# Evacuating L, T and Q of the RWKV chunk inverse with one VectorE operation over two PSUM banks

## What is computed

```python
def wkv7(r, decay, k, v, kk, a):          # per head: state is 64 x 64
    def step(state, inp):
        r_t, w_t, k_t, v_t, kk_t, a_t = inp
        sa = jnp.einsum('bhvk,bhk->bhv', state, kk_t)
        state = (state * w_t[:, :, None, :]
                 - sa[..., None] * (kk_t * a_t)[:, :, None, :]
                 + v_t[..., None] * k_t[:, :, None, :])
        y = jnp.einsum('bhvk,bhk->bhv', state, r_t)
        return state, y
```

## Time and profile before

| what | us |
|---|---|
| median of 3 runs | 4954.84 |
| lowest and highest | 4953.95, 4960.62 |
| the profiled execution | 4947.15 |
| its span, first to last instruction | 4945.4 |
| PE busy in it | 4560.1 |
| DVE busy in it | 1713.5 |
| ACT busy in it | 1292.5 |
| POOL busy in it | 339.9 |

### The profile page before, as it was taken

One profiled execution on the slowest core, in us unless ns is written; L12 is line 12 of the kernel. 1 busy time (PEld: TensorE's weight loads), 2 busy tenths in 40 slices (PEclk: granted clock), 3 DMA queues, 4 the chain that ended last, 5 costly groups with the idle time before them and its releaser, 6 DMA issues.

```text
span 4945.4 us, 91370 instructions
## 1 busy us (share of the span) xinstructions
PE 4560.1 (92%) x36311; PEld 2445.3 (49%) x36311; DVE 1713.5 (35%) x3522; ACT 1292.5 (26%) x2794; POOL 339.9 (7%) x466
## 2 busy tenths in 40 slices
PE   6999999999999999999999998994999999999992
PEld 4455555555555555555555555453444444444440
DVE  3334444444444344344344344224111111111115
ACT  4222332332232333323323332431111111111115
POOL 0000000000000000000000000000000000000004
PEclk8999999999999999999999999996999999999996
DMA  8101001001001001001001002333788888888887
GB/s 295 50 5 47 10 8 47 10 8 47 10 10 45 10 12 43 10 12 45 8 12 45 8 12 69 107 123 132 281 330 335 339 330 340 333 330 343 330 322 296
DMA packets 252843, 637.03 MB, mean 129 GB/s; under 512 B 11026, under 2 KB 96244, under 8 KB 252532
## 3 DMA queue, kind: packets, MB, share of 16 engines
q1 hardware_dynamic: 238852, 582.26, 32.3%
q0 software_dynamic: 13680, 49.81, 2.6%
HBM read 563.32 MB, written 68.71 MB: 128 GB/s over the span
## 4 chain that ended last, share of the span: by engine, by line
PE 88%; issue 4%; DVE 3%; DMA 2%; SPq 1%; POOL 1%; ACT 1%; DVEq 0%; POOLq 0%; ACTq 0%
PE bank L892 36%; PE bank L1216 18%; PE bank L1235 9%; PE bank L1104 5%; PE duo L1015 4%; PE duo L1002 2%; PE duo L1004 2%; PE bank L933 1%; PE duo L1205 1%; PE duo L984 1%; PE bank L947 1%; PE duo L829 1%; DMA yb<-y_s,dix 1%; DVE LTb L1847 1%; PE duo L1156 1%
## 5 line engine op out<-in xcount | busy, mean ns | idle before, releaser
L892 PE MATMUL bank<-hT,w 128*128 (+1 forms) x4096 | 1790.5, 594 | 0.0
L892 PEld LDWEIGHTS bank<-hT,w 128*128 128x128 f32 x4096 | 777.9, 191 | 994.0 <-issue 994.0
L1216 PE MATMUL bank<-WI,xT 128*128 128x512 f32 x2016 | 877.8, 594 | 2.4 <-DVE xT L2068 2.4
L1216 PEld LDWEIGHTS bank<-WI,xT 128*128 128x128 f32 x2016 | 379.2, 191 | 455.9 <-issue 455.9
L1235 PE MATMUL bank<-WO,aT 128*128 128x512 f32 x1008 | 443.1, 593 | 1.0 <-DVE ysb L2085 1.0
L1262 ACT ACT_TABLE_LOAD x268 | 343.8, 1283 | 20.9 <-DVE ub L1812 14.3
L2074 DVE TENSOR_TENSOR gsig<-bank,gsig 128x512 f32<-128x512 f32 x63 | 43.6, 692 | 847.6 <-ACT gsig L1262 847.6
L1235 PEld LDWEIGHTS bank<-WO,aT 128*128 128x128 f32 x1008 | 186.8, 190 | 212.5 <-issue 211.2
L1262 ACT ACTIVATE gsig<-bank 128x512 f32<-128x512 f32 x63 | 37.6, 598 | 827.8 <-PE bank L1216 827.8
L1015 PE MATMUL duo<-Qm,Zm 64*64 64x64 f32 x5120 | 203.6, 227 | 36.4 <-issue 29.6
L659 POOL TENSOR_TENSOR Tm<-Tm,idents 128x512 f32<-128x512 f32 x32 | 40.6, 1268 | 2842.9 <-DVE Tm L1845 2842.9
(11 more groups left out here) (338 smaller groups left out, 5313.2 us busy)
## 6 DMA issues: line engine op xcount, KB each, us to landing
WI<-in_w_expert_in_dram SPq DMA_DIRECT2D x63, 4096.0 KB, 17.0
WO<-in_w_expert_out_dram SPq DMA_DIRECT2D x63, 2048.0 KB, 7.9
w<-in_w_in_dram SPq DMA_DIRECT2D x64, 512.0 KB, 3.9
y_s<-ysb SPq DMA_DIRECT2D x63, 512.0 KB, 17.7
adaw<-in_w_ada_dram SPq DMA_DIRECT2D x12, 2048.0 KB, 13.0
xt<-in_x_dram SPq DMA_DIRECT2D x16, 512.0 KB, 9.2
WAc<-rank_s SPq DMA_DIRECT2D x32, 256.0 KB, 3.2
GDc<-rank_s SPq DMA_DIRECT2D x32, 256.0 KB, 3.2
```

Of the source, the lines that this page charges most:

```text
L892: ins = mm(PJ[j % 2][:, :], w[:, j, k, :], hT[:, k, ds(group(i) * G, G)], start=k == 0, stop=k == KT - 1)
L1216: ins = mm(GU[j][:, :], xT[:, s, k, :], WI[:, s, k, j * DE:j * DE + DE], start=k == 0, stop=k == KT - 1)
```

## The change

`evacuate` keeps only LT and GK. L, Z, T and Q go through a new `evacuate_both`, one operation of 128x512 over both banks, which signals by adding 2. A hop behind the product is then made by the general clause, that is behind the whole evacuation.

```diff
                 def evacuate(kind, lv, b):
                     u = (kind, lv, b, 0)
                     wait_gram(dve, i, u)
...
-                    if kind == "L":
-                        ins = V.tensor_tensor(Tm[:, cs, :], bk, over(m0s[:, :], 4), ALU.mult)
...
-                    elif kind == "T":
-                        ins = V.tensor_tensor(Tm[:, cs, :], Tm[:, cs, :], bk, ALU.subtract)
                     else:
-                        ins = V.tensor_tensor(Qm[p][:, cs, :], Qm[p][:, cs, :], bk, ALU.subtract)
-                    ins.then_inc(S["gram_evac"], 1)
...
+                def evacuate_both(kind, lv):
+                    u = (kind, lv, 1, 0)
+                    wait_gram(dve, i, u)
+                    bk = DUO[pair_of(u)][:, :, 0:4 * HD].rearrange("p b (c t) -> p b c t", t=HD)
+                    to = {"L": Tm, "Z": Zm, "T": Tm, "Q": Qm[p]}[kind][:, :, :].rearrange("p (b c) t -> p b c t", b=2)
+                    if kind in ("L", "Z"):
...
+                        ins = V.tensor_tensor(to, to, bk, ALU.subtract)
+                    ins.then_inc(S["gram_evac"], 2)
...
-                        if name == "Z":
-                            evacuate_Z(more[0])
+                        if name not in ("LT", "GK"):
+                            evacuate_both(name, more[0])
                         else:
                             evacuate(name, more[0], 0)
                             if SCHED[n + 1][0] == "hop":
```

More of the change, by code:

```diff
@@ L1841, in evacuate @@
                     wait_gram(dve, i, u)
-                    bk = bank(u)[:, 0:4 * HD].rearrange("p (c t) -> p c t", t=HD)
-                    cs = slice(4 * b, 4 * b + 4)
-                    if kind == "L":
-                        ins = V.tensor_tensor(Tm[:, cs, :], bk, over(m0s[:, :], 4), ALU.mult)
[L1846 to L1849, removed]
-                    elif kind == "T":
-                        ins = V.tensor_tensor(Tm[:, cs, :], Tm[:, cs, :], bk, ALU.subtract)
-                    else:
-                        ins = V.tensor_tensor(Qm[p][:, cs, :], Qm[p][:, cs, :], bk, ALU.subtract)
@@ L1854, in evacuate @@
-                    ins.then_inc(S["gram_evac"], 1)
[L1856 to L1862, removed]
+                    V.tensor_tensor((LTb if kind == "LT" else GKb)[p][:, 4 * b:4 * b + 4, :],
+                                    bank(u)[:, :].rearrange("p (c t) -> p c t", t=P),
+                                    over(mN[:, :], 4), ALU.mult).then_inc(S["gram_evac"], 1)
@@ new lines, in evacuate_both @@
+                def evacuate_both(kind, lv):
[4 more added lines that the diff above has]
+                    if kind in ("L", "Z"):
+                        mask = m0s[:, :] if kind == "L" else mlevs[:, lv - 1, :]
+                        ins = V.tensor_tensor(to, bk, mask.unsqueeze(1).unsqueeze(1).to_broadcast([P, 2, 4, HD]),
+                                              ALU.mult)
+                    else:
+                        ins = V.tensor_tensor(to, to, bk, ALU.subtract)
+                    ins.then_inc(S["gram_evac"], 2)
```

## The result

| what | before | after |
|---|---|---|
| median, us | 4956.56 (18 runs) | 4968.77 (18 runs) |
| lowest to highest, us | 4948.46 to 4960.62 | 4960.64 to 4978.54 |
| the profiled execution, us | 4947.15 | 4966.49 |
| DVE busy, us | 1713.5 | 1680.4 |
| PE busy, us | 4560.1 | 4558.5 |

The ratio is 1.0027, with a 95% interval of 1.0021 to 1.0034: 12 us slower, where 15 were forecast. On another chip the same kernel came out at 1.0041 [1.0028, 1.0054]. VectorE has 33 us less to do, and the kernel is slower by a quarter of a per cent or more.

A forecast was written before the change was run, and what follows sets the result against it. PE was taken to bound the kernel, waiting for hops' `xs` rather than evacuations. Terms 0.26 + 0.23 + 0 - 0.01 = 0.48 us a step, over 31 steps 14.9 us, put the median at 4970 (+0.3%), range 4957 to 4981.

The forecast's parts named there:

- Place 1, L/x0: Hop x0 behind L's evacuation: u0 waits for `xs`, so it starts 0.26 us later; term 0.26 us a step.
- That the delay stays: From u0 through LT to u1: DVE has no pause up to `xs` of x1, so the whole chain moves by 0.26.
- Place 5, Q3/x5: Hop x5 behind Q3's evacuation: u5 bound, +0.27, partly refunded by a gap; term 0.23 between 0.04 and 0.27.
- T4's gap: "Issue" gap of 0.23 us in product T4; if it ends at a fixed time, T4 and x6 move less.
- Places 2, 3, 4, 6, 7: Hops at T1/x2, Q2/sy3, T3/sy4, T4/x6 and Q5/sy7: slack or cover, term 0 each; T4/x6 bounded by 0 and 0.26.
- the pairs without a hop: Three merged pairs with no hop between: each saves 0.06 us on DVE, given 0.01 together.
- place 6: Hop x6 behind T4's evacuation: u6 held by Q4 if place 5 made that late; term 0, bounds 0 and 0.26.
- The gaps take it back: Rival: PE's "issue" gaps shorten and refund half of the delay, no measurable change, 4962.5 us; chance 0.22.
- More places are bound: Rival: places 2, 3 and 6 join where gaps fall otherwise, 25 us slower, 4980 us; chance 0.16.
- The saved cost counts: Rival: PE waits for DVE's evacuations, so 320 pairs by 0.06 give 19 us less, 4936 us; chance 0.05.
- Step 0: The step without hops: gains at most ten times 0.06 us, left out of the sum.

The follow-up runs named there:

- hop_first: The changed kernel, but with the hop put ahead of the merged evacuation at L/x0, Q3/x5 and T4/x6; ratio to the kernel before 0.9987 [0.9978, 0.9996].
- merge_others: The changed kernel, but with halves and the hop between them at L/x0 and Q3/x5 only; ratio to the kernel before 0.9998 [0.9989, 1.0007].
- merge_nohop: The changed kernel, but merged at T2, Q1 and Q4 alone, with halves and the hop between at the seven places; ratio to the kernel before 0.9991 [0.9982, 1.0].
- before_add_one: The kernel before the change, with Z's evacuation adding 1 to its semaphore in place of 2; 4933.29 against 4940.14 us, ratio 0.9983 [0.9974, 0.9992].

## Why the prediction was right, and where its sizes were off

- **What bounds.** Right. `xs` is what PE waits for, and the saving on DVE was no time: its busy time fell and the kernel became slower.
- **Place 1, L/x0.** Right place, mis-sized term: 0.37 for 0.26. The part that was worked out from rows holds: u0 came 1.06 us behind the start of L's evacuation (1.05 forecast), `xs` of x1 4.71 behind it (4.74 forecast). What failed is the silent assumption that the merged operation starts when the half did. It waits for the second signal (0.03 to 0.04) and for the separate wait instruction that comes with adding 2 (0.07).
- **That the delay stays.** Right result, by a chain that was not complete. "From there DVE has no pause" is true in the rows, but the length of DVE's seeds is set by GpSimd's. For a delay it made little difference (0.37 at `xs` of x0, 0.33 at that of x1): L's evacuation is also complete sooner, 1.55 in place of 1.90, and GpSimd's work on T with it. GpSimd's first seed then starts 0.24 us later and DVE's 0.37, so that DVE's is hardly held and takes 0.42 us in place of 0.45, which is the 0.03. For a gain it would have been wrong: hop_first lost all of it there.
- **Place 5, Q3/x5.** Right, mis-sized: from x5 to u5 it is 1.25 us in place of 0.87, so +0.38 where the sum had 0.23 between 0.04 and 0.27. The refund that I expected from T4's gap isn't there (u5 +0.79, Q4 +0.78), and the upper bound of 0.27 was too low for the same reason as at place 1.
- **Places 2, 3, 4, 6, 7 and the pairs without a hop.** Right, by merge_others and merge_nohop. `xs` of x4 still stood 0.73 us behind Z3's evacuation, and x4 alone was late. u6 starts 0.86 us behind the start of Q4 before and after, so it is Q4 that holds it. The condition that I gave, that place 5 has already made Q4 late, is needed: in merge_others, where it hasn't, place 6 costs 0.09.
- **The sum.** 0.48 a step was forecast, 0.78 measured in the profiled execution and 0.65 in its repetition (31.37 less 30.72), which by 31 steps is 24 and 20 us. That the forecast time fits the first median so closely (4970 for 4968.77) is partly luck: the sum was too small, and something outside the steps' table made up for it. In the profiled execution this is the start, faster by 4.4 us, and the dense parts, by 2.0 (1893.1 in place of 1895.1); for the medians it isn't shown. The second comparison, 18.4 us, is the one that comes near the table. Why the two medians' differences, 12.2 and 18.4, are apart isn't settled.
- **DVE's busy time** fell by 33 us and not by 46. I took 320 times 0.14 from durations alone. But three pairs of ten stand back to back and save 0.06 each, as my own part on the edit's cost says: 96 by 0.06 and 224 by 0.14 are 37 us. The two numbers of the prediction contradicted each other.
- **The wait for `xs`** rose by 20 us, and by 18 in the repetition, above the 8 to 15 given, in line with the dearer places.
- **The rivals.** "The gaps take it back" did happen on a small scale: from u3 to sy3 the delay falls from 0.46 to 0.35. At the two bound places nothing is taken back: u1 is as late as u0 within 0.03, and Q4 as late as u5. "More places are bound" fell with merge_others. "The saved cost counts" was not wholly empty either, in a way I had not weighed: 0.07 us of the start of Z's evacuations was worth 0.17% in before_add_one. Products and hops both stand behind these, and which of them gained is not told apart.
- **Step 0** was left out as at most 0.6 us of gain. It took 1.0 us more in the profiled execution (22.42 against 21.41) and 0.1 in the repetition; whatever this is, it isn't the merging.

## What to carry to other kernels

Fewer and larger operations on an engine are no gain where another waits for something queued behind them: read who is waited for, and place the short, waited-for operation ahead of the long one or between two halves. When one operation takes the place of two, price its start as well as its length: which signal it awaits and how that wait is issued. And if an operation that you freed still ends at the same time, look at what the neighbour engine does beside it, since the first operation's end may be the neighbour's.

## What the runs showed of the hardware that I had not expected

- A DVE operation that adds 2 to its semaphore has its wait issued as a separate instruction, and starts 92 to 94 ns behind the signal; one that adds 1, of the same size over the same two banks, starts 22 to 24 ns behind it. Whether this is the chip or the way the program is built, the runs don't tell; the effect on the time is 0.17% in before_add_one.
- DVE's 64x256 operations on two SBUF tiles took 0.42, 0.45, 0.69 and 0.85 us on average, by how far a like operation of GpSimd beside them had come. Those that were held ended some 0.28 us behind it, and in the first seeds this was so for two starts 0.25 us apart, while GpSimd's own first one took 0.72 us in all these cases. Over the span, the mean of DVE's 64 seeds was 652 ns before, 637 after and 767 with the hop ahead of L:

```profile
L1863 DVE TENSOR_TENSOR Qm<-LTb,m0Ts 64x256 f32<-64x256 f32 x64 | 40.8, 637 | 1.5
```

```profile
L1873 DVE TENSOR_TENSOR Qm<-LTb,m0Ts 64x256 f32<-64x256 f32 x64 | 49.1, 767 | 1.5
```
